# Two weight units in halves at the opening, squares folded between weight splits, and another order of ScalarE and VectorE in the scan and the last feed-forward pair

## The chip, the cores and the metric

The kernel runs on one core of a Trainium2 chip. The metric is the device time of one execution in microseconds. The kernel before was timed three times: 883.58, 883.80 and 884.14 us, median 883.8 us.

## The reference

Two transformer blocks over 256 tokens of width 1024, all in float32. The change touches only the first block, its opening, its scan and its feed-forward part; in the second block it renames semaphores.

```
h = rms_norm(x, norm_mix_pre);  z = h @ w_in
zq, zf_f, zf_b, zi, zg, zu, zv, ga, gb = split(z)

# scan mixer, both directions, 8 heads of 128
q = silu(zq);  v = zi
f = lb + (1 - lb) * sigmoid(zf);   k = (1 - lb) * sigmoid(-zf)
S_t = diag(f_t) S_{t-1} + k_t v_t^T;   o_t = S_t^T q_t
a = rms_norm(o_fwd + o_bwd) * silu(zg)

# spatial gating: tokens mixed inside chunks of 128
b = gelu(zu) * (w_s @ layer_norm(gelu(zv)) + b_s)

merged = sigmoid(ga) * (a @ w_a) + sigmoid(gb) * (b @ w_b)
x = x + rms_norm(merged @ w_out)
h2 = rms_norm(x)
x = x + rms_norm((silu(h2 @ w_gate) * (h2 @ w_up)) @ w_down)
x = x + (p @ w_ple) * sigmoid(x @ w_ple_gate)
```

The second block follows: an input projection, two attentions, an output projection and a feed-forward part with a squared relu.

## The kernel before, in words

**Units.** All weights stream through four slots of `raw` as units of 128 x 2048 floats (1 MB). ScalarE copies each unit to `whi` in the matmul's shortened float type (`split_hi`, L425), VectorE writes the rest `raw - whi` to `wlo` (`split_lo`, L834), and TensorE makes each product three times: high by high, low by high, high by low (`mm3`, L1523 to L1525, 48 matmuls of 256 columns per unit). SyncE loads unit u+4 as soon as unit u's last matmul has counted up `unit_used`. ScalarE and VectorE split three units ahead (`ahead(u)` splits u+3). The order on each engine is the order in which its block of code is written; nothing is scheduled.

**Opening.** SyncE sends the parameters, the first half of x, unit 0 in two halves, the second half of x and then whole units. ScalarE and VectorE make high and low parts of the gained x (`gained_hi` L450, `gained_lo` L883) and of the halves of unit 0 (L472, L913). TensorE multiplies unit 0 in two halves (`first_products`, L1631 to L1637) and then unit 1 (L1650 to L1652): 48 matmuls of 512 columns in all. ScalarE squares x (L478), VectorE folds the eight tiles of squares to one (`fold`, L867), TensorE sums them over partitions (`norm_stats`, L1613), GpSimd raises to the power -0.5 (L338), VectorE spreads the factors (L862), and TensorE broadcasts them (`norm_bc`, L1619). After that unit 2 and the further ones follow (`two_tiles`). A chain of small VectorE instructions normalises zv (from L940) for `spatial_mix` (L1666), which stands between units 4 and 5. GpSimd issues four loads (lnr, sgw, sgb, lvl) once unit 1 has landed.

**Scan.** Units 4 to 15 give q, f and k for two groups of four heads (g = 0 and 1). The scan is a tree of levels: for each level ScalarE copies alternating key rows to `Kc` (`both_ways`, L506), TensorE multiplies them with the queries (L1692), VectorE selects the results into S (L988) and multiplies the decays into the queries (`tree_update`, L964 and L970), and GpSimd does so to the keys (`keys_update`, L354). `prep` on VectorE makes the key sum `ksum` (L977), which level 0 (L1680) and the first Kc copy need, and the first decayed queries (L980). Level 8 is the last (L1699).

**Feed-forward.** Eleven pairs of hidden tiles: a gate unit, an up unit and a down unit each. For a pair VectorE scales the gate (L1138), ScalarE takes silu (L614), VectorE multiplies by the factors and by the up result (L1145, L1150), ScalarE and VectorE split the hidden tile (L618, L1154), and TensorE multiplies it by the down unit (L1776 to L1778). The splits of three coming units stand between these steps. Behind the last pair come copies and mean squares of the token-major results and a diagonal of factors (L1087, L1098), which the turning matmuls use (L1781).

Of the kernel before, what the change touches and what calls it, by code (L numbers as in the profile page):

```python
# [172 lines left out]
def build_blocks(nc, w, xT, pT, par, cst, lvl, sgw, sgb, lnr, rel, oneh, maskb, pos, out):  # L173
    scratch = nc.dram_tensor("bias_scratch", [HEADS, 512], F32, kind="Internal").ap()
    ctx = ExitStack()
    with ctx:
# [84 lines left out]
        zi = view(72, 8, D)  # L261
        t1 = view(80, 4, 512)
# [43 lines left out]
        def _(sp):  # L306
            sp.dma_start(par_s[:, :], par).then_inc(sem("par_in"), 16)
            sp.dma_start(x[:, 0:4, :], xT[:, 0:4, :]).then_inc(sem("x_in"), 16)
            for half in range(2):
                cols = slice(half * UNIT // 2, (half + 1) * UNIT // 2)  # L310
                sp.dma_start(raw[:, 0, cols], w[stored(0)][:, cols]).then_inc(sem(f"raw_half{half}"), 16)
            sp.dma_start(x[:, 4:8, :], xT[:, 4:8, :]).then_inc(sem("x_in2"), 16)
# [11 lines left out]
        def _(pool):  # L324
            pool.dma_start(cst_s[:, :], cst).then_inc(sem("cst_in"), 16)
            pool.wait_ge(sem("raw_in1"), 16)
# [3 lines left out]
            pool.dma_start(lvl_s[:, :, :], lvl).then_inc(sem("lvl_in"), 16)  # L330
            nc.gpsimd.memset(half_s[:, :], -0.5).then_inc(sem("half"), 1)
            pool.wait_ge(sem("half"), 1)
# [7 lines left out]
            token_factors(0)  # L340

# [48 lines left out]
            def head_factors(name, a, n):  # L390

                pool.wait_ge(sem(name + "_eps"), 1)
                nc.gpsimd.tensor_tensor(rh[:, a:a + n], ms[:, a:a + n], half_s[:, 0:1].broadcast_to([P, n]), ALU.pow)\
                    .then_inc(sem(name + "_fac"), 1)
                pool.wait_ge(sem(name + "_fac"), 1)
# [13 lines left out]
            for j in range(4):  # L409
                rotate(j)  # L410
                head_factors(f"sq{j}", 48 + 4 * j, 4)
# [6 lines left out]
        def _(act):  # L418
            A = nc.scalar.activation

            def split_hi(u):

                slot = u % SLOTS
                act.wait_ge(sem(f"raw_in{slot}"), 16 * (u // SLOTS + (slot > 0)))
# [39 lines left out]

            act.wait_ge(sem("par_in"), 16)
            act.wait_ge(sem("x_in"), 16)
            for k in range(2):
                gained_hi("n1", "mix_pre", 0, k)
            for half in range(2):
                cols = slice(half * UNIT // 2, (half + 1) * UNIT // 2)  # L470
                act.wait_ge(sem(f"raw_half{half}"), 16)
                A(whi[:, 0, cols], raw[:, 0, cols], ACT.Copy).then_inc(sem(("first_hi", "hi_ready")[half]), 1)  # L472
# [152 lines left out]
            for j in range(1, PAIRS1):  # L625
# [191 lines left out]
        def _(dve):  # L817
# [88 lines left out]

            dve.wait_ge(sem("par_in"), 16)
            dve.wait_ge(sem("x_in"), 16)
            for half in range(2):
                cols = slice(half * UNIT // 2, (half + 1) * UNIT // 2)  # L910
                gained_lo("n1", "mix_pre", 0, half)
                dve.wait_ge(sem(("first_hi", "hi_ready")[half]), 1)
                V.tensor_tensor(wlo[:, 0, cols], raw[:, 0, cols], whi[:, 0, cols].bitcast(F32), ALU.subtract)\  # L913
                    .then_inc(sem(("first_lo", "lo_ready")[half]), 1)
            dve.wait_ge(sem("x_in2"), 16)
            for k in range(2, 4):
                gained_lo("n1", "mix_pre", 0, k)
            split_lo(1)
            dve.wait_ge(sem("norm_sq"), 2)
            fold(sq1)  # L920

            gam = par_s[:, PAR["gamma"]:PAR["gamma"] + 16]
            V.tensor_tensor(lb[:, 0, :], gam, gam, ALU.subtract).then_inc(sem("gam_sub"), 1)
# [1413 lines left out]
```

## Time and profile before

| what | us |
|---|---|
| median of three timed runs | 883.8 |
| the profiled execution itself | 882.76 |
| its span, first to last instruction | 881.0 |
| TensorE busy (matmul) | 859.0 (98%) |
| VectorE busy | 581.9 (66%) |
| ScalarE busy | 443.7 (50%) |
| GpSimd busy | 91.9 (10%) |

A timeline row gives the start, the length, the engine, the line, the operation, what is written and read, the shape and the number of instructions merged in the row; in square brackets stands how long the engine had been idle before it and what ended that. A float32 product (not in the shortened type) leaves two matmul records each in the trace.

### The profile page before, as it was taken

The numbers are of one execution on the slowest core, as the hardware profiler recorded it, in microseconds if no ns is written. First come the engines' busy times: TensorE is split into PE (matmuls) and PEld (weight loads), VectorE is DVE, ScalarE is ACT, GpSimd is POOL, SyncE is SP. The second block draws the span as 40 slices with busy tenths as digits, with TensorE's granted clock in tenths as the row PEclk, the third lists the DMA queues.
The fourth block names the chain that finished last, engine by engine and source line by source line (L and its number), as shares of the span: only waits on it lengthen the run. The fifth ranks groups of instructions, "written<-read, shape, count | busy, mean of one in ns | idle before, by whom it ended". The sixth has DMA issues, their size and how long they took to land. (4 is left out here: it accounts for less than half of the span.)

```text
span 881.0 us, 15077 instructions
## 1 busy us (share of the span) xinstructions
PE 859.0 (98%) x6628; PEld 826.1 (94%) x6628; DVE 581.9 (66%) x703; ACT 443.7 (50%) x516; POOL 91.9 (10%) x71
## 2 busy tenths in 40 slices
PE   5999999999999999999999999999999999999997
PEld 4999998999999899999999899998998999999997
DVE  5866896676676587555565687688787765555454
ACT  6578764553344475344333564466556644444440
POOL 1000541452000000000000001000441000000000
PEclk9999999999999999999999999999999999999999
DMA  9554344244355455555555536544221455555551
GB/s 334 191 183 151 137 144 142 98 144 144 109 191 176 148 203 172 177 184 189 187 191 192 184 124 225 164 176 144 97 96 50 164 176 187 191 191 176 171 180 49
DMA packets 21121, 143.90 MB, mean 163 GB/s; under 512 B 2578, under 2 KB 2594, under 8 KB 4416
## 3 DMA queue, kind: packets, MB, share of 16 engines
q1 hardware_dynamic: 20016, 139.51, 45.4%
q0 software_dynamic: 1040, 3.43, 1.1%
q8 instruction: 52, 0.85, 0.4%
q14 instruction: 13, 0.11, 0.0%
HBM read 141.87 MB, written 1.06 MB: 162 GB/s over the span
## 5 line engine op out<-in xcount | busy, mean ns | idle before, releaser
L1523 PE MATMUL ps<-xh,whi 128*128 128x256 f32 x1656 | 475.4, 287 | 1.3 <-DVE wlo L834 1.0
L1524 PE MATMUL ps<-xl,whi 128*128 128x256 f32 x1656 | 468.9, 283 | 0.0
L1525 PE MATMUL ps<-xh,wlo 128*128 128x256 f32 x1656 | 468.8, 283 | 0.0
L834 DVE TENSOR_TENSOR wlo<-raw,whi 128x2048 fp32r<-128x2048 f32 x130 | 297.4, 2290 | 133.7 <-ACT whi L425 133.0
L425 ACT ACTIVATE whi<-raw 128x2048 fp32r<-128x2048 f32 x130 | 247.9, 1910 | 165.6 <-DMA raw<-w 165.5
L1523 PEld LDWEIGHTS ps<-xh,whi 128*128 128x128 f32 x1656 | 317.8, 192 | 4.4 <-issue 1.7
L1524 PEld LDWEIGHTS ps<-xl,whi 128*128 128x128 f32 x1656 | 317.9, 192 | 0.5
L1525 PEld LDWEIGHTS ps<-xh,wlo 128*128 128x128 f32 x1656 | 317.7, 192 | 0.0
L354 POOL TENSOR_TENSOR work<-work 128x512 f32<-128x512 f32 x28 | 55.5, 2001 | 126.2 <-ACT work L506 99.4
L618 ACT ACTIVATE xh<-work 128x512 fp32r<-128x512 f32 x27 | 17.1, 632 | 81.0 <-DVE work L1486 41.2
L893 DVE TENSOR_TENSOR work<-ps,bcs 128x512 f32<-128x512 f32 x34 | 23.4, 689 | 21.9 <-PE ps L1525 20.0
L1776 PE MATMUL ps<-whi,xh 128*128 128x512 f32 x88 | 34.5, 392 | 0.8 <-DVE xl L1154 0.8
L1777 PE MATMUL ps<-whi,xl 128*128 128x512 f32 x88 | 34.4, 391 | 0.0
L1778 PE MATMUL ps<-wlo,xh 128*128 128x512 f32 x88 | 34.3, 389 | 0.0
L456 ACT ACTIVATE work<-work 128x512 f32<-128x512 f32 x26 | 16.4, 631 | 29.6 <-DVE work L893 29.4
L1154 DVE TENSOR_TENSOR xl<-work,xh 128x512 fp32r<-128x512 f32 x27 | 18.7, 693 | 18.8 <-ACT xh L618 18.8
L1692 PE MATMUL ps<-work 128*128 128x128 f32 x224 | 29.4, 285 | 1.0 <-ACT work L506 1.0
L1692 PEld LDWEIGHTS ps<-work 128*128 128x128 f32 x224 | 28.1, 192 | 1.4 <-ACT work L506 1.2
L370 POOL TENSOR_TENSOR nt<-nt,half_s 128x1 f32<-128x1 f32 x4 | 2.2, 552 | 250.6 <-DVE nt L1093 250.6
L988 DVE COPY_PREDICATED work<-lvl_s,ps 128x512 f32<-128x512 int32 x28 | 19.1, 739 | 13.6 <-PE ps L1692 12.6
L338 POOL TENSOR_TENSOR rtok<-eps_s,half_s 128x2 f32<-128x2 f32 (+1 forms) x5 | 3.9, 770 | 225.8 <-DVE eps_s L860 225.8
L883 DVE SCALAR_TENSOR_TENSOR xl<-x,par_s,xh 128x256 fp32r<-128x256 f32 x32 | 13.9, 481 | 10.3 <-ACT xh L450 10.3
(264 smaller groups left out, 927.0 us busy)
## 6 DMA issues: line engine op xcount, KB each, us to landing
raw<-w SPq DMA_DIRECT2D x130, 1024.0 KB, 4.9
x<-xT SPq DMA_DIRECT2D x2, 512.0 KB, 6.7
raw<-w SPq DMA_DIRECT2D x2, 512.0 KB, 7.6
work<-bias_scratch POOLq DMA_DIRECT2D x1, 1024.0 KB, 7.8
out<-x SPq DMA_DIRECT2D x4, 256.0 KB, 2.3
work<-lnr POOLq DMA_DIRECT2D x1, 512.0 KB, 6.0
work<-sgw POOLq DMA_DIRECT2D x1, 512.0 KB, 6.7
lvl_s<-lvl POOLq DMA_DIRECT2D x1, 448.0 KB, 9.2
```

Source lines behind the costliest of these rows:

```text
L354: ins = nc.gpsimd.tensor_tensor(v, v, pair[:, :, 1 - d:2 - d].broadcast_to([P, n, half]), ALU.mult)
L425: A(whi[:, slot, :], raw[:, slot, :], ACT.Copy).then_inc(sem("hi_ready"), 1)
L834: V.tensor_tensor(wlo[:, slot, :], raw[:, slot, :], whi[:, slot, :].bitcast(F32), ALU.subtract)\
L893: V.tensor_tensor(dst, two(ps[u % RING][:, :]), factors_by_tile(2), ALU.mult).then_inc(sem(f"evac{u % RING}"), 1)
L988: V.copy_predicated(H["S"][:, s, :, s * P:(s + 1) * P], lvl_s[:, lv - 1, :].unsqueeze(1).broadcast_to([P, 4, P]), ps[3 + 2 * g + s][:, :]. ...
L1523: mm(out, hi, xh[:, tile, :], start=start, stop=False, skip_group_check=skip)
L1524: mm(out, hi, xl[:, tile, :], start=False, stop=False, skip_group_check=skip)
L1525: return mm(out, wlo[:, slot, at:at + width], xh[:, tile, :], start=False, stop=stop, skip_group_check=skip)
L1692: last = mm(banks[s][:, h * P:(h + 1) * P], H["Kc"][:, h, s * P:(s + 1) * P], alternating(H["Q"], lv, 1, h * T + s * P, P), start=True, st ...
L1776: mm(o, xh[:, base + kk, xs], whi[:, slot, wc], start=first, stop=False, skip_group_check=True)
L1777: mm(o, xl[:, base + kk, xs], whi[:, slot, wc], start=False, stop=False, skip_group_check=True)
L1778: return mm(o, xh[:, base + kk, xs], wlo[:, slot, wc], start=False, stop=end, skip_group_check=True)
```

## The change

The opening:

- the parameters are loaded by ScalarE's DMA queue, x is SyncE's first load, and unit 1, too, comes in two halves;
- VectorE sets 128 x 128 elements of `work` to one, ScalarE runs a one-element Copy and TensorE 26 float32 products of that tile with itself into a bank that nobody reads, before anything has landed;
- TensorE multiplies both units by `first_products`, in four quarters ordered by part (high, low of x, low of the weights);
- VectorE splits unit 1 in halves; its fold of the squares is cut in two around the split of unit 2; the split of unit 3 comes ahead of the norm's factors;
- `norm_stats` moves from between units 1 and 2 into the middle of unit 2;
- GpSimd's loads of lnr, sgw and sgb wait for unit 3 instead of unit 1, and lvl comes behind the norm's factors and unit 4;
- ScalarE loads the Gelu table by a one-element Gelu before the split of unit 4.

The scan: `ksum` is a step of its own. For group 0 VectorE scales unit 10 before the splits of units 12 and 13, and ScalarE makes the first Kc copy before it activates unit 10. For group 1 VectorE does the decayed queries after the seventh level of group 0 instead of before it.

The feed-forward part: in the last pair both engines split the second of the three coming units behind the hidden tile instead of ahead of it.

In the second block several semaphores become one with a count (`sq`, `red`), with the same waits.

```diff
 sync
-            sp.dma_start(par_s[:, :], par).then_inc(sem("par_in"), 16)
             sp.dma_start(x[:, 0:4, :], xT[:, 0:4, :]).then_inc(sem("x_in"), 16)
-            for half in range(2):
...
-            for u in range(1, UNITS):
+            for u in range(2):
+                for half in range(2):
+                    cols = slice(half * UNIT // 2, (half + 1) * UNIT // 2)
+                    sp.dma_start(raw[:, u, cols], w[stored(u)][:, cols]).then_inc(sem(f"raw_half{2 * u + half}"), 16)
+                if u == 0:
+                    sp.dma_start(x[:, 4:8, :], xT[:, 4:8, :]).then_inc(sem("x_in2"), 16)
+            for u in range(2, UNITS):
 gpsimd
-            pool.wait_ge(sem("raw_in1"), 16)
+            nc.gpsimd.memset(half_s[:, :], -0.5).then_inc(sem("half"), 1)
+            pool.wait_ge(sem("half"), 1)
+            pool.wait_ge(sem("raw_in3"), 16)
...
-            pool.dma_start(lvl_s[:, :, :], lvl).then_inc(sem("lvl_in"), 16)
...
             token_factors(0)
+            pool.wait_ge(sem("raw_in0"), 16)
+            pool.dma_start(lvl_s[:, :, :], lvl).then_inc(sem("lvl_in"), 16)
 scalar
+            act.dma_start(par_s[:, :], par).then_inc(sem("par_in"), 16)
+            act.wait_ge(sem("warm_set"), 1)
+            A(warm[:, :], wtile[:, 0:1], ACT.Copy)
...
-            split_hi(1)
+            first_hi(1)
             for k in range(2):
                 A(sq1[:, 4 * k:4 * k + 4, :], x[:, 4 * k:4 * k + 4, :], ACT.Square).then_inc(sem("norm_sq"), 1)
             split_hi(2)
+            split_hi(3)
...
-            ahead(U_ZV)
-            ahead(U_ZV + 1)
-            filled(U_ZV + 1)
+            act.wait_ge(sem("half"), 1)
+            A(warm[:, :], half_s[:, 0:1], ACT.Gelu)
+            split_hi(4)
...
-                    if kind == "level" and 1 <= lv <= 7 and (g, lv) != (1, 1):
+                    if kind == "level" and 1 <= lv <= 7 and lv + g > 1 and (g, lv) != (1, 1):
                         both_ways(g, lv)
                 if not U_ZI <= u < U_GA:
                     ahead(u)
+                if u == U_Q[1]:
+                    both_ways(0, 1)
...
                 silu_pair(j)
-                split_hi(u + 1 + RING)
+                if j < PAIRS1 - 1:
+                    split_hi(u + 1 + RING)
                 hidden_hi(j, "hid", 2 * (j % 2), j % 2)
+                if j == PAIRS1 - 1:
+                    split_hi(u + 1 + RING)
 vector
+            V.memset(wtile, 1.0).then_inc(sem("warm_set"), 1)
...
+            link(V.tensor_tensor(sq1[:, 0:4, :], sq1[:, 0:4, :], sq1[:, 4:8, :], ALU.add))
             split_lo(2)
+            link(V.tensor_tensor(sq1[:, 0:2, :], sq1[:, 0:2, :], sq1[:, 2:4, :], ALU.add))
+            V.tensor_tensor(sq1[:, 0, :], sq1[:, 0, :], sq1[:, 1, :], ALU.add).then_inc(sem("folded"), 1)
+            split_lo(3)
+            norm_factors("n1", 0)
+            split_lo(4)
...
                 if u == U_Q[1] - 1:
                     gates(0, 1, 1)
+                    hgrn_dve("ksum", 0, 0)
                     hgrn_dve("prep", 0, 0)
+                    scaled(U_Q[1], G[1]["q"][:, 0:2, :])
                 for step in behind.get(u, ()):
                     hgrn_dve(*step)
+                if u == U_ZI + 1:
+                    hgrn_dve("prep", 1, 0)
                 ahead(u)
...
                 if u == U_ZI:
-                    hgrn_dve("prep", 1, 0)
+                    hgrn_dve("ksum", 1, 0)
 tensor
+            pe.wait_ge(sem("warm_set"), 1)
+            for _ in range(26):
+                mm(ps[3][:, 0:P], wtile, wtile, start=True, stop=True)
             first_products(0)
             used(first_products(1))
-            arrived(U_ZV + 1)
...
+            first_products(2)
+            used(first_products(3))
             pe.wait_ge(sem("cst_in"), 16)
-            norm_stats("n1", sq1)
...
+                    if u == U_ZU:
+                        steps.append(lambda: norm_stats("n1", sq1))
```

VectorE at the opening, before; `xl` and `wlo` are low parts, `work` holds the squares, `lb` the scan's lower bounds:

```order
L883 SCALAR_TENSOR_TENSOR xl<-x,par_s,xh 128x256 x4
L834 TENSOR_TENSOR wlo<-raw,whi 128x2048
L867 TENSOR_TENSOR work<-work 128x1024
L867 TENSOR_TENSOR work<-work 128x512
L867 TENSOR_TENSOR work<-work 128x256
L923 TENSOR_TENSOR lb<-par_s 128x16
L834 TENSOR_TENSOR wlo<-raw,whi 128x2048
```

The same place now:

```order
L931 TENSOR_TENSOR wlo<-raw,whi 128x1024
L942 TENSOR_TENSOR lb<-par_s 128x16
L944 TENSOR_TENSOR work<-work 128x1024
L850 TENSOR_TENSOR wlo<-raw,whi 128x2048
L946 TENSOR_TENSOR work<-work 128x512
L947 TENSOR_TENSOR work<-work 128x256
L850 TENSOR_TENSOR wlo<-raw,whi 128x2048
L876 TENSOR_SCALAR eps_s<-ps 128x2
L878 COPY rx<-rtok 128x256
L850 TENSOR_TENSOR wlo<-raw,whi 128x2048
```

The split of unit 2 (the first 128x2048 row) now stands inside the fold, and that of unit 3 ahead of the norm's factors.

ScalarE in the scan at units 9 to 11, before; the 128x4x128 row copies level 0 out of PSUM, and the 128x1024 row behind it is the first Kc copy:

```order
L425 ACTIVATE whi<-raw 128x2048
L456 ACT_TABLE_LOAD
L456 ACTIVATE work<-work 128x512
L514 ACTIVATE work<-ps 128x4x128 x2
L506 ACTIVATE work<-work 128x1024
L425 ACTIVATE whi<-raw 128x2048
```

The same place now:

```order
L428 ACTIVATE whi<-raw 128x2048
L517 ACTIVATE work<-work 128x1024
L459 ACT_TABLE_LOAD
L459 ACTIVATE work<-work 128x512
L525 ACTIVATE work<-ps 128x4x128 x2
L428 ACTIVATE whi<-raw 128x2048
```

The Kc copy moved ahead of the table load, of the activation of unit 10 and of the copies of level 0.

VectorE in the last feed-forward pair, before; the 128x512 rows are the hidden tile's steps, the first L1087 row is the first copy behind the pair:

```order
L1138 TENSOR_TENSOR work<-ps,bcs 128x512
L834 TENSOR_TENSOR wlo<-raw,whi 128x2048 x2
L1145 TENSOR_TENSOR work<-work,bcs 128x512
L1150 TENSOR_TENSOR work<-work,ps 128x512
L1154 TENSOR_TENSOR xl<-work,xh 128x512
L834 TENSOR_TENSOR wlo<-raw,whi 128x2048
L1087 COPY work<-ps 128x512
```

The same place now:

```order
L1168 TENSOR_TENSOR work<-ps,bcs 128x512
L850 TENSOR_TENSOR wlo<-raw,whi 128x2048
L1175 TENSOR_TENSOR work<-work,bcs 128x512
L1180 TENSOR_TENSOR work<-work,ps 128x512
L1184 TENSOR_TENSOR xl<-work,xh 128x512
L850 TENSOR_TENSOR wlo<-raw,whi 128x2048 x2
L1117 COPY work<-ps 128x512
```

One weight split changed sides of the hidden tile's three steps.

## Rows read from the trace of the kernel before

**Rows 1.** The page, part 1: busy time of each engine.
```profile
PE 859.0 (98%) x6628; PEld 826.1 (94%) x6628; DVE 581.9 (66%) x703; ACT 443.7 (50%) x516; POOL 91.9 (10%) x71
```

**Rows 2.** Timeline of TensorE, from the first product to unit 5.
```profile
10.05 2.05 PE L1631 MATMUL ps<-whi,xh 128*128 128x512 f32 x4 [10.05 <-ACT whi L472]
...
14.84 1.09 PE L1631 MATMUL ps<-whi,xh 128*128 128x512 f32 x4
...
18.15 0.50 PE L1650 MATMUL ps<-whi,xh 128*128 128x512 f32 x1 [0.39 <-DVE wlo L834]
...
23.72 0.50 PE L1613 MATMUL ps<-cst_s,work 128*128 128x1 f32 x4
...
30.29 0.37 PE L1523 MATMUL ps<-xh,whi 128*128 128x256 f32 x1
...
41.98 1.97 PE L1666 MATMUL ps<-work 128*64 128x128 f32 x32
```

**Rows 3.** Timeline of the other engines at the opening.
```profile
0.74 0.38 SPq L307 DMA_DIRECT2D par_s<-par  x1
1.18 0.42 SPq L308 DMA_DIRECT2D x<-xT  x1
...
8.87 1.04 ACT L472 ACTIVATE whi<-raw 128x1024 fp32r<-128x1024 f32 x1
...
13.85 1.92 ACT L425 ACTIVATE whi<-raw 128x2048 fp32r<-128x2048 f32 x1 [0.77 <-DMA raw<-w]
...
15.68 1.99 ACT L478 ACTIVATE work<-x 128x1024 f32<-128x1024 f32 x2
...
18.01 2.40 DVE L867 TENSOR_TENSOR work<-work 128x1024 f32<-128x1024 f32 x3
...
29.95 1.41 DVE L940 BATCH_NORM_STATS2 nt<-work 128x6 f32<-128x512 f32 x2
...
38.03 0.69 DVE L893 TENSOR_TENSOR work<-ps,bcs 128x512 f32<-128x512 f32 x1
```

**Rows 4.** The page, part 6: the load of lnr, size and time to landing.
```profile
work<-lnr POOLq DMA_DIRECT2D x1, 512.0 KB, 6.0
```

**Rows 5.** Windows: behind the last product; TensorE's granted clock stands last but two.
```profile
878.00:881.00 3.00, 0.00 (x0) 0.00 (x0) 0.00 (x0) 0.00 (x0) 0.00 (x0) 0.50 0.24 90
```

**Rows 6.** Timeline of the scan of group 0, units 9 to 11.
```profile
77.88 1.23 DVE L977 TENSOR_TENSOR work<-work 128x1024 f32<-128x1024 f32 x1
79.02 2.35 DVE L980 TENSOR_TENSOR work<-work 128x1024 f32<-128x1024 f32 x2
...
79.89 1.28 ACT L456 ACT_TABLE_LOAD   x1
...
85.70 1.52 ACT L506 ACTIVATE work<-work 128x1024 f32<-128x1024 f32 x1
...
87.27 2.92 PE L1692 MATMUL ps<-work 128*128 128x128 f32 x16 [1.04 <-ACT work L506]
```

**Rows 7.** Timeline at the end of group 0's levels.
```profile
130.79 5.14 POOL L354 TENSOR_TENSOR work<-work 128x512 f32<-128x512 f32 x2 [2.93 <-DVE work L970]
...
132.95 2.07 DVE L977 TENSOR_TENSOR work<-work 128x1024 f32<-128x1024 f32 x1
134.94 3.20 DVE L980 TENSOR_TENSOR work<-work 128x1024 f32<-128x1024 f32 x2
...
140.81 0.60 PE L1699 MATMUL ps<-work 128*128 128x128 f32 x3 [0.36 <-DVE work L964]
```

**Rows 8.** Timeline of the last feed-forward pair and what follows.
```profile
491.91 2.29 DVE L834 TENSOR_TENSOR wlo<-raw,whi 128x2048 fp32r<-128x2048 f32 x1 [3.15 <-ACT whi L425]
...
497.12 0.47 PE L1776 MATMUL ps<-whi,xh 128*128 128x512 f32 x1 [0.76 <-DVE xl L1154]
...
501.88 0.29 DVE L1098 TENSOR_SCALAR work<-cst_s,nt 128x128 f32<-128x128 f32 x1
...
502.65 1.95 PE L1781 MATMUL ps<-work 128*128 128x128 f32 x16
```

More of the change, by code:

```diff
@@ L462, in bc_copy, with first_hi @@
                 A(bcs[:, :], ps[7][:, T:2 * T], ACT.Copy).then_inc(sem("norm_bcs"), 1)
+            act.dma_start(par_s[:, :], par).then_inc(sem("par_in"), 16)
+            act.wait_ge(sem("warm_set"), 1)
+            A(warm[:, :], wtile[:, 0:1], ACT.Copy)
             act.wait_ge(sem("par_in"), 16)
             act.wait_ge(sem("x_in"), 16)
+            def first_hi(u):
+                for half in range(2):
+                    cols = slice(half * UNIT // 2, (half + 1) * UNIT // 2)
+                    act.wait_ge(sem(f"raw_half{2 * u + half}"), 16)
+                    A(whi[:, u, cols], raw[:, u, cols], ACT.Copy).then_inc(sem(("first_hi", "hi_ready")[half]), 1)
             for k in range(2):
                 gained_hi("n1", "mix_pre", 0, k)
[L469 to L472, printed above, removed]
+            first_hi(0)
             act.wait_ge(sem("x_in2"), 16)
@@ L975, in hgrn_dve @@
                 H = G[g]
+                if kind == "ksum":
+                    V.tensor_tensor(H["ksum"], H["K"][0], H["K"][1], ALU.add).then_inc(sem("ksum"), 1)
                 if kind == "prep":
-                    V.tensor_tensor(H["ksum"], H["K"][0], H["K"][1], ALU.add).then_inc(sem("ksum"), 1)
                     activated(U_Q[g] + 1)
@@ L1630, in first_products @@
                 for s, k in pairs:
-                    mm(o[s], xh[:, k, xs[s]], whi[:, 0, 512 * k:512 * k + 512], start=k == 0, stop=False)
-                pe.wait_ge(sem("act_lo"), half + 1)
+                    mm(o[s], xh[:, 2 * quarter + k, xs[s]], whi[:, u, wc[k]], start=quarter == 0 and k == 0, stop=False)
+                pe.wait_ge(sem("act_lo"), quarter + 1)
                 for s, k in pairs:
-                    mm(o[s], xl[:, k, xs[s]], whi[:, 0, 512 * k:512 * k + 512], start=False, stop=False)
@@ L1635, in first_products @@
-                pe.wait_ge(sem(("first_lo", "lo_ready")[half]), 1)
+                    mm(o[s], xl[:, 2 * quarter + k, xs[s]], whi[:, u, wc[k]], start=False, stop=False)
+                pe.wait_ge(sem(("first_lo", "lo_ready")[half]), u + 1)
                 for s, k in pairs:
-                    last = mm(o[s], xh[:, k, xs[s]], wlo[:, 0, 512 * k:512 * k + 512], start=False, stop=False)
+                    last = mm(o[s], xh[:, 2 * quarter + k, xs[s]], wlo[:, u, wc[k]], start=False, stop=quarter == 3 and k == 1)
@@ L1638, in first_products @@
                 return last
+            pe.wait_ge(sem("warm_set"), 1)
+            for _ in range(26):
+                mm(ps[3][:, 0:P], wtile, wtile, start=True, stop=True)
             first_products(0)
             used(first_products(1))
-            arrived(U_ZV + 1)
-            for s in range(2):
-                o = ps[(U_ZV + s) % RING][:, :]
-                for k in range(4):
-                    if s == 0 and k % 2 == 0:
-                        pe.wait_ge(sem("act_lo"), before("lo", "n1") + 3 + k // 2)
-                    xs = slice(s * P, (s + 1) * P)
-                    wc = slice(512 * k, 512 * k + 512)
-                    mm(o, xh[:, 4 + k, xs], whi[:, 1, wc], start=False, stop=False)
-                    mm(o, xl[:, 4 + k, xs], whi[:, 1, wc], start=False, stop=False)
-                    last = mm(o, xh[:, 4 + k, xs], wlo[:, 1, wc], start=False, stop=k == 3)
@@ L1653, in _ @@
-            used(last)
+            first_products(2)
+            used(first_products(3))
             pe.wait_ge(sem("cst_in"), 16)
-            norm_stats("n1", sq1)
             inside, behind = hgrn_schedule()
```

75 lines of the change are left out of this document (35 added, 40 removed).

## The prediction

> **What bounds the kernel now.** I read the page's busy times first. TensorE has matmuls in flight for 859.0 of 881.0 us, VectorE and ScalarE are far below that [rows 1]. So an edit pays only where it lets TensorE start sooner, run at a higher clock or not stand still, and the timeline of TensorE is the view to go by: what stands in its square brackets is all there is to win, apart from slow products. TensorE's first product starts at 10.05; from 14.84 on groups of four take 1.09 us instead of 2.05; it waits briefly at 18.15 [rows 2]. Then it waits for ScalarE's first Kc copy at 87.27 [rows 6], for VectorE at level 8 at 140.81 [rows 7] and for the last pair's hidden tile at 497.12 [rows 8]. These four places are the ones that the change touches. The idle time in a row is a little less than the loss: the four products at 14.84 take 1.09, while 24 products from 18.15 to 23.72 come 0.232 apart [rows 2], so a record lasts 1.09 - 3 x 0.232 = 0.39, or 0.16 beyond its spacing. I add 0.16 to each idle time. The weights arrive whenever a unit is used up, so loads move with TensorE and take nothing back; later stages move with it as a whole.
>
> **The start.** x was the second load, issued at 1.18; now it is the first, at 0.74 [rows 3]: 0.44 us. ScalarE copied the first half unit at 8.87 for 1.04 us [rows 3] and TensorE began 0.14 later. The x parts and the table load, which the one-element Copy puts into the empty wait, are then long done, so the landing decides, and I let it move by the 0.44: first product at 9.6. Bounds: 0 (the loads compete anyway, and the parameters now run on another queue beside x) to 1.0 (the half was not waited for, so it may have landed before 8.87).
>
> **The clock.** TensorE had done nothing before 10.05. The twelve products up to 14.84 would take 2.8 us at 0.232 and took 4.79; with slow ones at twice 0.232 that makes 8.7 slow products, about 4.0 us at 1.2 GHz and a loss of 2.0 [rows 2]. The new 26 products are float32, eight of which (16 records) take 1.95 [rows 8], so about 0.22 each, 0.44 at the lower level. If they start at about 1.1 (the first loads are issued at 0.74, and a small memset comes first), 4.0 us make 9 of them, and the other 17 take 3.7: done at 8.8, ahead of 9.6. So they cost nothing and give back the 2.0. Bounds: 2.0 gained to about 3 lost, the latter below. As to the time between 8.8 and 9.6: in this trace the granted clock is at 0.50, the 1.2 GHz level, in the window from 878 to 881, in which TensorE has no product [rows 5]. The Trainium skill's page "TensorE: Matmul & The Clock Gate", section "Part 1: The HAM clock gate (the "warmup" mystery)", says that the throttled state is the default and that activity releases it; by that rule the slow products at 10.05 and the low clock at the end are one thing, and warm products help as long as the pause behind them is short.
>
> **The opening's sum.** 48 products of two units at 0.232 take 11.1 us: from 9.6 to 20.7, without a wait, since the halves' copies (1.04 each) and VectorE's halves keep ahead of quarters of 2.8 us each. Unit 2 must be split by then. Unit 1 landed at 13.85, so its second half lands at 13.4; behind the first half's copy ScalarE has it at about 14.7. The squares take 1.99, the copy of unit 2 1.92 [rows 3]: 18.6. VectorE's split takes 2.29 [rows 8]: 21.0 with a signal. The fold used to stand as one piece of 2.40 [rows 3]; cut in two, its first part lies in the wait for that copy. So unit 2 starts at 21.0, a wait of 0.3. From 23.72 to 30.29 lay norm_stats, unit 2 and norm_bc, 6.57 [rows 2]; the same three are there now in another order: unit 3 at 27.6 instead of 30.29. **Gain 2.7.** Without the move of norm_stats it would wait for the second part of the fold; in the middle of unit 2, at 23.9, the fold (done at about 22.2) is ready. Bounds of the opening: 0.7 (start not earlier, products slow) to 3.7.
>
> What is late next: the zv chain on VectorE. It began at 29.95 behind two splits, so the factors were done 4.6 earlier, 1.65 behind the start of norm_stats at 23.72 [rows 2, 3]. Now: 23.9 + 1.65, one split of 2.29, about 0.9 for the four lower-bound steps that were ahead before: 28.8. From 29.95 to the scaling at 38.03 it took 8.1 [rows 3], so it ends at 36.9. spatial_mix, at 41.98 [rows 2] less 2.7, wants it at 39.3. Room 2.4, cost nothing. GpSimd's loads now wait for unit 3 (about 18.5: unit 1 at 13.4 and two units of some 2.5 us each); lnr took 6.0 [rows 4], so it is there at 24.5, ahead of 28.8. Those on lvl are needed only at 87.
>
> **The scan.** ksum ends at 79.1, ScalarE is free at 79.89 (where the table load starts), and the copy takes 1.52 [rows 6]: Kc at 81.4 instead of 87.22. The table load, 1.28, moves behind it to 82.7, the queries are decayed by 81.4, and level 0's copies come in time, as they did just before 85.70. TensorE is at level 1 at 87.27 - 1.04 - 0.16 = 86.07 and finds all. **Gain 1.2**; bounds 0 and 1.2. At the end of group 0, 3.20 us of decayed queries for group 1 [rows 7] leave from ahead of the seventh selection, which then ends around 137.8; GpSimd's last keys are done at 130.79 + 5.14 = 135.9, TensorE comes at 140.3. **Gain 0.36 + 0.16 = 0.5**; bounds 0 and 0.5. The moved queries are wanted only after unit 20.
>
> **The last pair.** VectorE's split at 491.91 takes 2.29 and waited for a landing; the hidden tile stood behind it. Now the tile's steps start with the up unit's end and are done at about 493, TensorE wants them at 497.12 - 0.76 - 0.16 = 496.2. The gain is 0.92, if the next chain follows: the diagonal was ready at 501.88 + 0.29 = 502.17 and used at 502.65 [rows 8], room 0.48, and the second split now stands next to the third ahead of it. Both fit, since the third waits for its load anyway. **Gain 0.85**, bounds 0.48 and 0.92. The renamed semaphores have the same waits: 0.
>
> **Sum.** 2.7 + 1.2 + 0.5 + 0.85 = 5.25 us. The profiled execution, 882.76 with 1.8 around its span, becomes 877.5. The median of the timed runs is 1.0 above the profiled one, so I predict 883.8 - 5.25 = 878.6.
>
> **Rivals.**
>
> *The first products are slow all the same* (the clock has fallen again by 9.6, or rises late). For it: nothing in the trace shows the clock across a pause of a microsecond or two at the start, and it is low without products [rows 5]. Against it: the pause is short. 48 products end at 9.6 + 11.1 + 2.0 = 22.7, unit 3 starts at 29.3, gain 1.0, total 3.55: 880.3.
>
> *The 26 products run at 1.2 GHz to their end.* Then 26 x 0.44 = 11.4, end at 12.5, and the real ones finish between 23.6 and 25.6; unit 3 starts at 30.2 to 32.2, a gain of 0.1 to a loss of 1.9. With the middle, -0.9, the total is 1.65: 882.2. Against it: the clock rose after 4 us in the opening before.
>
> *The scan hands its wait on.* GpSimd's first keys now run from 81.4 beside VectorE's splits of units 12 and 13. Side by side, the key sum took 2.07 instead of 1.23 and the queries 3.20 instead of 2.35, and GpSimd 5.14 [rows 6, 7]. The split of unit 12 could go from 82.0 to 84.3 and must be done by 87.8, so a stretch of 0.85 is harmless, and I keep 1.7 for the scan; if it isn't, because selections start late level after level, the 1.7 is lost: 880.3. The Trainium skill's page "SBUF — State Buffer", section "SBUF: two separate sides", has VectorE with two SBUF inputs and GpSimd exclude each other for a whole instruction; by that rule the split would wait up to one of GpSimd's two key steps, half of 5.14, and end at 86.9, still in time but 0.9 from the edge.
>
> *Slower: lnr lands late.* Its load is issued later than before, next to units 4 and 5. Each microsecond of landing beyond 28.8 + 2.4 = 31.2 holds up the zv chain and, at spatial_mix, TensorE. The kernel is slower by what can be told from 38.3 on (31.2 + 5.25 + 1.8), that is if 0.5 MB take 20 us and not 6.0 [rows 4]; at 40 it is 883.8 - 5.25 + 8.8 = 887.3. Nothing speaks for that length, as the queue's megabytes come in about 2.5 us each.
>
> **Numbers.** Forecast with its mechanism, 877.8 to 879.4: 0.62. Slow first products 0.10, the scan's wait handed on 0.10, slow warm products 0.05, late lnr 0.02. The rest, 0.11, is halves of the terms' bounds: an earlier start than 9.6 (down to 877) or none, and small new waits (up to 881). Range 877.2 to 881.0; below and above it about 0.1 each. This kernel's time is told from no change at about 0.2%, 1.8 us: faster 0.93, same 0.05, slower 0.02.
>
> **What would show it.** The first product at 9.6 and four of them in 1.09 already; no wait among the four quarters; unit 2 at 21.0, unit 3 at 27.6; spatial_mix 2.7 earlier without a wait; no idle time at level 1, level 8 and in the last down unit; the turning products at most 0.1 late. Wrong would be: groups of 2.05 again, a start above 10, VectorE as releaser of unit 2 by more than 1 us, a wait at a later level, or the end less than 4.5 us earlier although those waits are gone.

## Result and profile after

The new kernel takes 876.13 us (median of 4 runs, 875.93 to 876.31) against 883.69 us for the kernel before, timed beside it: ratio 0.992, 95% interval 0.9908 to 0.9932, 7.6 us less. Forecast were 878.6 with a range from 877.2, so direction and places were right and the gain was 2.3 us too small. Its profiled execution took 875.93 with a span of 874.1: 6.8 us less than the profiled execution before.

The page's busy times, to be held against [rows 1]:

```profile
PE 863.9 (99%) x6680; PEld 832.1 (95%) x6680; DVE 583.5 (67%) x705; ACT 445.1 (51%) x519; POOL 93.9 (11%) x71
```

TensorE is busy 4.9 us longer in a span 6.8 us shorter: the products of ones fill 7.6 us that were idle, and the slow products at the start, about nine by the prediction's own working, are gone. The timeline of TensorE at the opening, answering to [rows 2]:

```profile
1.06 7.64 PE L1671 MATMUL ps<-work 128*128 128x128 f32 x52 [1.06 <-DVE work L923]
8.62 1.16 PE L1660 MATMUL ps<-whi,xh 128*128 128x512 f32 x4
...
11.43 1.07 PE L1660 MATMUL ps<-whi,xh 128*128 128x512 f32 x4
...
18.68 1.07 PE L1666 MATMUL ps<-wlo,xh 128*128 128x512 f32 x4
...
23.09 0.50 PE L1639 MATMUL ps<-cst_s,work 128*128 128x1 f32 x4
...
38.45 1.97 PE L1687 MATMUL ps<-work 128*64 128x128 f32 x32
```

The real products start at 8.62, four take 1.16 or 1.07 us from the first group on, and no idle time stands among the quarters. The other engines there, answering to [rows 3]:

```profile
0.74 0.40 ACTq L468 DMA_DIRECT2D par_s<-par  x1
0.74 0.38 SPq L308 DMA_DIRECT2D x<-xT  x1
...
5.20 1.71 ACT L453 ACTIVATE xh<-x,par_s 128x256 fp32r<-128x256 f32 x4 [2.53 <-DMA par_s<-par]
...
7.42 1.06 ACT L479 ACTIVATE whi<-raw 128x1024 fp32r<-128x1024 f32 x1 [0.51 <-DMA raw<-w]
...
17.70 2.29 DVE L850 TENSOR_TENSOR wlo<-raw,whi 128x2048 fp32r<-128x2048 f32 x1 [0.35 <-ACT whi L428]
...
20.14 0.36 PE L1549 MATMUL ps<-xh,whi 128*128 128x256 f32 x1 [0.38 <-DVE wlo L850]
...
26.77 0.36 PE L1549 MATMUL ps<-xh,whi 128*128 128x256 f32 x1
```

ScalarE now really waits for the first half unit (0.51) and starts its copy at 7.42 instead of 8.87. That needs the early table load too: its parts of x run from 5.20 to 6.9, and with the 1.28 us of the table load [rows 6] ahead of them they would have ended at 8.2, an estimate from these rows. Unit 2 waits 0.38 + 0.16 for its split; unit 3 starts at 26.77 instead of 30.29, 3.5 us earlier.

In the scan (answering to [rows 6, 7]) and behind the last pair ([rows 8]), the same timeline:

```profile
82.55 2.83 PE L1713 MATMUL ps<-work 128*128 128x128 f32 x16
...
135.48 0.72 PE L1720 MATMUL ps<-work 128*128 128x128 f32 x5
...
496.12 0.29 DVE L1128 TENSOR_SCALAR work<-cst_s,nt 128x128 f32<-128x128 f32 x1
...
496.55 2.02 PE L1804 MATMUL ps<-work 128*128 128x128 f32 x16 [0.22 <-DVE work L1128]
```

Levels 1 and 8 start without idle time, 4.7 and 5.3 us earlier than before. The last down unit has none either, but the turning products wait 0.22 + 0.16 for the diagonal.

TensorE's instructions, set side by side one by one in the two traces, give the account of the 6.8 us:

| place | forecast | found |
|---|---|---|
| opening, up to unit 3 | 2.7 | 3.5 |
| scan, levels 1 and 8 | 1.7 | 1.9 |
| last pair | 0.85 | 0.6 (1.0 less 0.45 at the turning products) |
| the rest, up to the last product | 0 | -0.1 |
| from the last product to the end of the span | 0 | 0.9 |

The remaining 0.7 us of the 7.6 is not between the two traces: the timed runs of the kernel before have their median 0.9 above its profiled run, those of the new one 0.2.

The traces show what the last row of the table goes with. The DMA view of the last output's transfer, from its issue to its landing, in the kernel before (877.4 to 880.6):

```profile
q14 instruction: 1, 0.01, 0.6%
out<-x SPq DMA_DIRECT2D x1, 256.0 KB, 3.2
```

with the scan's edits alone (875.1 to 877.7; the run is told of below):

```profile
q14 instruction: 1, 0.01, 0.7%
out<-x SPq DMA_DIRECT2D x1, 256.0 KB, 2.6
```

and in the new kernel (871.5 to 873.8), whose view has no line of `instruction` there:

```profile
q1 hardware_dynamic: 169, 0.28, 32.7%
out<-x SPq DMA_DIRECT2D x1, 256.0 KB, 2.3
```

One packet of 8 KB that loads instructions runs 0.31 us in the middle of the last output's transfer. Packet by packet, it starts 1.83 us behind the issue in the kernel before, and the output's last 4-byte packet comes only behind it, at 2.13; the landing takes 3.18 us. With the scan or the pair alone that small packet gets in just ahead of it, and the landing takes 2.58. In all nine profiles with the new opening the nearest such packet stands 4.3 to 4.4 us ahead of the issue, and the landing takes 2.28 to 2.34. This holds in all 14 profiles. No edit moved that packet alone, and why it costs more than its 0.3 us is not shown.

### The profile page after: what moved, and what is told of

It is laid out like the page before. It is cut to its first block, busy times and chain, and to the rows that moved or that the text cites. A ratio compares the mean times of both kernels' runs of the same rounds, so it can differ in the third digit from the quotient of the medians.

```text
span 874.1 us, 15188 instructions
## 1 busy us (share of the span) xinstructions
PE 863.9 (99%) x6680; PEld 832.1 (95%) x6680; DVE 583.5 (67%) x705; ACT 445.1 (51%) x519; POOL 93.9 (11%) x71
## 4 chain that ended last, share of the span: by engine, by line
PE 86%; DVE 7%; ACT 4%; DMA 1%; issue 1%; SPq 0%; POOL 0%; DVEq 0%
PE ps L1549 22%; PE ps L1550 21%; PE ps L1551 21%; PE ps L1713 3%; PE ps L1800 2%; PE ps L1799 2%; PE ps L1801 2%; DVE wlo L850 2%; ACT whi L428 1%; PE ps L1615 1%; PE ps L1621 1%; PE ps L1618 1%; DMA x<-xT 1%; ACT work L732 1%; PE ps L1804 1%
## 5 line engine op out<-in xcount | busy, mean ns | idle before, releaser
L357 POOL TENSOR_TENSOR work<-work 128x512 f32<-128x512 f32 x28 | 57.3, 2067 | 119.0 <-DVE work L1004 52.8
L517 ACT ACTIVATE work<-work 128x1024 f32<-128x1024 f32 x14 | 16.1, 1147 | 8.2 <-POOL work L357 3.5
```

The lines of the kernel that those rows point to most:

```text
L357: ins = nc.gpsimd.tensor_tensor(v, v, pair[:, :, 1 - d:2 - d].broadcast_to([P, n, half]), ALU.mult)
```

## Experiments

The numbers below stand against the kernel before on the same chip; it had a median of 882.85 to 883.17 there, with runs from 881.6 to 885.7.

**The opening alone.** The new kernel with the scan's and the last pair's edits taken back, in the code of ScalarE and of VectorE:

```diff
-                if u == U_Q[1]:
-                    both_ways(0, 1)
...
-                if j < PAIRS1 - 1:
-                    split_hi(u + 1 + RING)
+                split_hi(u + 1 + RING)
                 hidden_hi(j, "hid", 2 * (j % 2), j % 2)
-                if j == PAIRS1 - 1:
-                    split_hi(u + 1 + RING)
...
-                    hgrn_dve("ksum", 0, 0)
                     hgrn_dve("prep", 0, 0)
-                    scaled(U_Q[1], G[1]["q"][:, 0:2, :])
...
```

> The new kernel with the scan and the last feed-forward pair in the old order: the opening (and the semaphore names) alone. Theory A (three independent places, and the rest of the 7.6 us is how long the last output took to land): first product at 8.6, norm_stats on TensorE about 3.5 us earlier than before, waits of 1.2 and 0.5 us in the scan and 0.9 at the last pair back in place; the end 3.5 us earlier, 880.2. Theory B (the opening gives its surplus to a later stage, or the shorter tail belongs to it): 879.3 or less, with the last output landing 2.3 us after its issue instead of 3.2.

Measured: 879.13 us (878.77 to 879.34), 3.7 less, ratio 0.9951 (0.9938 to 0.9964). TensorE's start:

```profile
1.06 8.83 PE L1656 MATMUL ps<-work 128*128 128x128 f32 x52 [1.06 <-DVE work L918]
9.64 1.17 PE L1645 MATMUL ps<-whi,xh 128*128 128x512 f32 x4
```

The waits in the scan and at the last pair are back (1.43, 0.51 and 1.14 us). The first product came at 9.64, not 8.6: the 26 products of ones took 1.2 us longer than in the new kernel, which at half rate means that the clock rose about 2.4 us later, and they ran until 9.6 although ScalarE's half was ready at 8.7. TensorE's lead on the kernel before is 3.1 us at unit 3 and 2.6 at the last product; the last output landed in 2.29 us. So theory B was right about the tail, which is 0.9 of the gain and belongs to this opening's program, and wrong about later stages, which got nothing.

**The scan alone.**

```diff
+                if u == U_Q[1]:
+                    both_ways(0, 1)
...
+                    hgrn_dve("ksum", 0, 0)
                     hgrn_dve("prep", 0, 0)
+                    scaled(U_Q[1], G[1]["q"][:, 0:2, :])
...
+                if u == U_ZI + 1:
+                    hgrn_dve("prep", 1, 0)
```

> The kernel before with the scan's new order alone. Theory A: the opening as before, no wait at level 1 and level 8, TensorE's last product 1.85 us earlier, time 881.9. Theory B (what shows as a scan gain needs the earlier VectorE of the new opening): 0.5 to 1.2 us, 882.5 to 883.2.

Measured: 880.56 us (879.81 to 881.01), 2.3 less, ratio 0.9968 (0.9955 to 0.9981). Both waits are gone with the old opening in place, against theory B. TensorE gains 1.95 us in the scan in this profile, near theory A's 1.85; the shorter landing of the last output (2.58 instead of 3.18) adds 0.6. The runs lie within 1.2 us of each other where the kernel before has 4.

**The last pair alone.** VectorE's part, ScalarE's is the same:

```diff
+                if j < PAIRS1 - 1:
+                    split_lo(u + 1 + RING)
                 hidden(j, j % 2, u + 1, (u + 1) % RING)
                 hidden_lo(j, j % 2, "hid", 0)
+                if j == PAIRS1 - 1:
+                    split_lo(u + 1 + RING)
```

> The kernel before with the last feed-forward pair's new order alone. Theory A: the wait of the last down unit (0.92) goes, one of about 0.35 appears at the turning products behind it, since VectorE's diagonal comes 0.35 late; net 0.6, 883.1. Rival: the diagonal is on time when the opening is the old one, net 0.9, 882.8.

Measured: 881.67 us, ratio 0.9992 (0.998 to 1.0003), no clear change; seven runs lie at 880.98 to 881.67 and five at 883.2 to 884.8. By itself this part cannot be told from the scatter by the times. In its trace the wait at the last down unit is gone and the turning products start 0.35 us late, a net 0.65, as theory A has it. Its profiled run, 883.22, is of the upper kind, and shows what one of these is:

```profile
88.17 3.70 PE L1698 MATMUL ps<-work 128*128 128x128 f32 x16 [2.38 <-ACT work L506]
```

```profile
80.00:87.50 7.50, 5.79 (x50) 5.58 (x48) 7.50 (x7) 3.76 (x6) 0.00 (x0) 1.00 0.41 139
88.25:91.66 3.41, 3.41 (x17) 3.41 (x17) 0.00 (x0) 2.19 (x2) 2.99 (x2) 0.50 0.50 209
```

The first row is the timeline's at level 1, the others are windows (TensorE's granted clock is the third number from the end). The wait for the first Kc copy is 2.5 us instead of 1.2 [rows 6], and behind it the clock is at 0.50, 1.2 GHz, for 3.41 us; the same 16 records take 3.70 instead of 2.92 us.

The longer wait has a source 25 us earlier. ScalarE's copy of one weight unit, in the kernel before, in its second profile (e10_before, below) and here:

```profile
61.14 1.90 ACT L425 ACTIVATE whi<-raw 128x2048 fp32r<-128x2048 f32 x1
```

```profile
62.33 1.92 ACT L425 ACTIVATE whi<-raw 128x2048 fp32r<-128x2048 f32 x1 [0.55 <-DMA raw<-w]
```

```profile
62.03 1.92 ACT L425 ACTIVATE whi<-raw 128x2048 fp32r<-128x2048 f32 x1 [1.25 <-DMA raw<-w]
```

The same load, issued at 55.7, 55.8 and 55.2, took 4.9, 6.5 and 6.8 us to land. TensorE did not notice, since the splits are three units ahead, but in e10_before VectorE stays 1.2 us behind the first profile from that unit's split to the scaling of unit 10, which ScalarE's activation and copies wait for ahead of the Kc copy. So the old order handed a late load on to level 1.

**The new kernel again,** unchanged, beside the three above.

> The new kernel once more, with its own profile, beside the kernel before. Theory A: TensorE's last product is again 5.9 us earlier than before's, while the landing of the last output varies between about 2.3 and 3.2 us from profile to profile; time 876.2 to 877.0, 6.5 to 7.6 us below the kernel before. Theory B (the short tail is the kernel's own): last landing 2.3 us again and 7.5 us below.

Measured: 876.09 us (875.90 to 876.17), 6.8 less, ratio 0.9916 (0.9902 to 0.9931). First product at 8.79; the last output landed in 2.29 us, as theory B has it, and the time lies between the two theories. One part alone gave 3.7, 2.3 and 1.2 by the medians (the last not to be told from none), 7.2 together, the whole 6.8. That they add up is in part luck: each has a shorter landing of the last output in it (0.9, 0.6 and 0.6 us), which the whole has once, the runs of the first were held up by the products of ones in its profile, and the kernel before scatters.

**The parameters ahead of x again.**

```diff
+            sp.dma_start(par_s[:, :], par).then_inc(sem("par_in"), 16)
             sp.dma_start(x[:, 0:4, :], xT[:, 0:4, :]).then_inc(sem("x_in"), 16)
...
-            act.dma_start(par_s[:, :], par).then_inc(sem("par_in"), 16)
```

> The new kernel with the parameters loaded by SyncE ahead of x again. Theory A (x second in the queue costs more than its issue time, since 128 small rows go ahead of it): x lands at 5.5 to 5.9 instead of 5.0, the first half unit at 8.2 to 8.8 instead of 7.5, first product at 9.5, time 877.0 (0.9 above the new kernel's 876.1). Rival (only the 0.44 us between the two issues counts): first product at 9.1, time 876.5.

Measured: 877.25 us (876.64 to 877.84), ratio 0.9929 (0.9914 to 0.9945) to the kernel before, 1.2 more than the new kernel. (The new kernel was timed on another chip than this and the next three; the kernel before has 882.89 on this one and 882.85 on that.) The copy of the first half and the first product:

```profile
8.65 1.06 ACT L479 ACTIVATE whi<-raw 128x1024 fp32r<-128x1024 f32 x1 [1.50 <-DMA raw<-w]
...
9.85 1.15 PE L1660 MATMUL ps<-whi,xh 128*128 128x512 f32 x4 [0.52 <-ACT whi L479]
```

A queue place of 0.43 us moved ScalarE's start on the first half by 1.2 (8.65 against 7.42 here; 7.3 to 7.7 in all seven other profiles with the parameters on ScalarE's queue). The half landed at 8.62 against 7.40; with the parameters ahead of x it lands at 8.2 to 8.8 in six profiles, without at 7.3 to 7.7 in eight. So the rival's 0.44 is too small, and theory A's price holds. Its reason, the small rows, is not shown: the edit moved the whole load, and nothing tells its size from its place.

**No products of ones, and ten of them.**

```diff
-            pe.wait_ge(sem("warm_set"), 1)
-            for _ in range(26):
-                mm(ps[3][:, 0:P], wtile, wtile, start=True, stop=True)
```

> The new kernel without the 26 products of ones on TensorE. Theory A (they buy the clock): the first product at 8.6 as now, some ten products twice as long, unit 2 starts 1.4 to 2 us later (a wait of 0.55 there is covered), time 877.5 to 878.1, and the runs spread by more than 0.5 us again. Rival (the granted clock rises soon anyway or unit 2's split binds): at most 876.8.

```diff
-            for _ in range(26):
+            for _ in range(10):
```

> The new kernel with 10 products of ones instead of 26, which end at about 5.2 and leave a pause of 3.4 us ahead of the first real product. Theory A (a short pause does no harm): 876.1 as with 26. Rival (the clock falls in the pause, the prediction's rival of slow first products): the first real products take 2.05 us per four, 877.5 to 878.1 as without any.

Measured: 877.59 us without (876.98 to 878.19), ratio 0.9933 (0.9917 to 0.9948), and 877.07 with ten (876.88 to 877.87), ratio 0.9928 (0.9911 to 0.9945); 1.5 and 1.0 more than with 26, and both scatter by 1 us. The intervals overlap that of 26 products (0.9902 to 0.9931), but all twelve runs lie above the nine with 26. TensorE without them:

```profile
8.73 2.04 PE L1660 MATMUL ps<-whi,xh 128*128 128x512 f32 x4 [8.73 <-ACT whi L479]
10.58 1.75 PE L1663 MATMUL ps<-whi,xl 128*128 128x512 f32 x4
12.17 1.09 PE L1666 MATMUL ps<-wlo,xh 128*128 128x512 f32 x4
```

and with ten:

```profile
1.06 4.64 PE L1671 MATMUL ps<-work 128*128 128x128 f32 x20 [1.06 <-DVE work L923]
8.81 2.05 PE L1660 MATMUL ps<-whi,xh 128*128 128x512 f32 x4 [3.11 <-ACT whi L479]
10.65 1.91 PE L1663 MATMUL ps<-whi,xl 128*128 128x512 f32 x4
12.36 1.62 PE L1666 MATMUL ps<-wlo,xh 128*128 128x512 f32 x4
13.81 1.09 PE L1660 MATMUL ps<-whi,xh 128*128 128x512 f32 x4
```

Ten products (4.64 us, the whole at the lower level) and a pause of 3.1 us left the real ones as slow as if there had been none: theory A of that run fell. But its rival is not shown either: the clock had not risen before the pause, so it could not fall in it. Whether ten were too few or the pause too long these runs cannot tell. The 26 buy about 1.5 us because the clock rises while they run. The Trainium skill's page "TensorE: Matmul & The Clock Gate", section "Part 1: The HAM clock gate (the "warmup" mystery)", calls the throttled state the default that activity releases; by that rule the slow groups here are expected, and these rows agree.

**norm_stats between units 1 and 2 again.**

```diff
             used(first_products(3))
             pe.wait_ge(sem("cst_in"), 16)
+            norm_stats("n1", sq1)
...
-                    if u == U_ZU:
-                        steps.append(lambda: norm_stats("n1", sq1))
```

> The new kernel with norm_stats between units 1 and 2 again. Theory A (the cut fold ends at 21.05): TensorE waits from 19.6 to 21.1 for the fold, unit 2 starts at 21.5 instead of 20.1 but holds no norm_stats, so 1.0 us is lost: 877.1. Rival (the wait for unit 2's split would have been there anyway and covers it): 876.3.

Measured: 877.11 us (876.89 to 877.89), ratio 0.9929 (0.9913 to 0.9944), 1.0 more than the new kernel.

```profile
9.59 1.17 PE L1660 MATMUL ps<-whi,xh 128*128 128x512 f32 x4
...
21.13 0.58 PE L1639 MATMUL ps<-cst_s,work 128*128 128x1 f32 x4 [0.39 <-DVE work L947]
```

Again the products of ones ran late, to 9.6; had the real ones started at 8.6, TensorE would only have waited longer for the fold, which follows from VectorE's split and not from TensorE, and ends at 21.0 in both programs. So the 1.0 us is the price of the place of norm_stats, as theory A has it.

**Filling the wait at level 1.** The kernel before, with five float32 products on a constant (ten records) ahead of TensorE's wait for Kc:

```diff
                     elif lv <= 7:
+                        if (g, lv) == (0, 1):
+                            idle_products(5, 5)
                         pe.wait_ge(sem("Kc"), 7 * g + lv)
```

> The kernel before, with five float32 products of the identity (1.1 us) into an idle bank while TensorE waits for the first Kc copy at level 1. They take nothing away and give no result. Theory A (the slower of the two clusters of the kernel before, 883.2 to 885.7 against 881.6 to 882.6, are executions in which the clock falls in that wait): the upper cluster goes, all runs within 1.5 us, median near 882.2 or below. Rival (the clusters come from the opening's slow products or the loads): two clusters as before.

**The kernel before, again.**

> The kernel before once more, with its own profile. Theory A: the first half unit lands at 8.2 to 8.8, first product 9.5 to 10.1, level 1's wait 1.2 to 2.5 us, and where the time is 883.2 or more the granted clock is 0.5 for 3.4 us there. Rival: the same wait in a slow and a fast execution, the difference in the opening.

Measured: with the filler 882.83 us (881.51 to 883.98, 11 runs), ratio 0.9993 (0.9984 to 1.0002), without it 883.95 (881.76 to 884.80, 12 runs) and 883.17 (881.81 to 885.51, 23 runs). Level 1 with the filler, then without:

```profile
85.66 1.28 PE L1607 MATMUL ps<-cst_s 128*128 128x128 f32 x10
86.99 2.92 PE L1694 MATMUL ps<-work 128*128 128x128 f32 x16
```

```profile
88.46 2.92 PE L1692 MATMUL ps<-work 128*128 128x128 f32 x16 [2.09 <-ACT work L506]
```

The two ratios show no clear change of time. But every run's mean granted clock is known. With the filler it is 0.999 or 1.000 in all 11 runs, and one of them is above 883.9 (883.98). Without it 13 of the 35 runs are above 883.9; their clock is 0.997 or 0.998 in 12 and 0.999 in the one that was profiled (883.96), while the runs up to 883.5 have 0.998 or more. The low clock behind the last product alone makes 0.998 [rows 5]; 0.997 stands in 12 of the 35 runs and in the profile with the fall at level 1. So falls of the clock go with most of the upper end, and none shows with the filler; that each of them is at level 1 is seen in one trace only. The filled kernel still spreads by 2.5 us where I had expected 1.5, and the profiled run at 883.96 has no fall, against theory A of that run: it has the long wait, 2.09 + 0.16, which is 1.05 of its 1.2 us above the first profile, and a clock that rose late in the opening, which is the other 0.15. Its first groups:

```profile
9.99 2.04 PE L1631 MATMUL ps<-whi,xh 128*128 128x512 f32 x4 [9.99 <-ACT whi L472]
11.83 1.91 PE L1634 MATMUL ps<-whi,xl 128*128 128x512 f32 x4
13.54 1.91 PE L1637 MATMUL ps<-wlo,xh 128*128 128x512 f32 x4
15.25 1.52 PE L1631 MATMUL ps<-whi,xh 128*128 128x512 f32 x4
```

Four groups are slow here, three in [rows 2]. Three things scatter the old kernel then, of which the new one shows none in its two profiles: the moment at which the clock rises, the length of the wait at level 1, and the fall behind it.

**Two further moves, with 26 and with 22 products of ones.**

```diff
-            for k in range(2):
-                A(sq1[:, 4 * k:4 * k + 4, :], x[:, 4 * k:4 * k + 4, :], ACT.Square).then_inc(sem("norm_sq"), 1)
+            A(sq1[:, 0:4, :], x[:, 0:4, :], ACT.Square).then_inc(sem("norm_sq"), 1)
             split_hi(2)
+            A(sq1[:, 4:8, :], x[:, 4:8, :], ACT.Square).then_inc(sem("norm_sq"), 1)
             split_hi(3)
...
+            split_lo(2)
             dve.wait_ge(sem("norm_sq"), 2)
             link(V.tensor_tensor(sq1[:, 0:4, :], sq1[:, 0:4, :], sq1[:, 4:8, :], ALU.add))
-            split_lo(2)
...
-                if j == PAIRS1 - 1:
-                    split_lo(u + 1 + RING)
-                split_lo(u + 2 + RING)
+                split_lo(u + (1 if j == PAIRS1 - 1 else 2) + RING)
...
             x_lo(3)
+            split_lo(U_PG + 1)
             ahead(U_PG - 1)
```

> The new kernel with two more moves: the second square of the first norm behind ScalarE's copy of unit 2 (and the fold's first step behind VectorE's split of it), and VectorE's split of unit 77 behind the turned results of the last pair. Theory A: the waits of 0.55 at unit 2 and 0.39 at the turning products go, 875.2 against 876.1. Rival (the fold is then late for norm_stats inside unit 2, or unit 77's split is late): 876.1 or more.

> The same with 22 products of ones instead of 26. Theory A (26 end after the first half unit is ready if the clock rises late, as in e1_open and e8_stats_between, and 22 don't): first product at 8.7 whatever the clock's moment, time as e11 where its clock rises early, up to 0.9 less where it rises late. Rival (the pause of 0.9 us lets the clock fall): 2 us more.

Measured: 875.49 us (875.18 to 876.09), ratio 0.9909 (0.9896 to 0.9922), and 875.19 us (875.09 to 875.21); the second, ratio 0.9905 (0.9892 to 0.9918) to the kernel before, is the best version by its median. The first is near theory A's 875.2. The timeline of the second:

```profile
1.06 6.54 PE L1670 MATMUL ps<-work 128*128 128x128 f32 x44 [1.06 <-DVE work L923]
8.79 1.17 PE L1659 MATMUL ps<-whi,xh 128*128 128x512 f32 x4 [1.19 <-ACT whi L479]
...
19.89 0.36 PE L1548 MATMUL ps<-xh,whi 128*128 128x256 f32 x1
...
495.92 1.95 PE L1803 MATMUL ps<-work 128*128 128x128 f32 x16
```

Both waits are gone, and a pause of 1.2 us after 22 products leaves the real ones at full rate, against the rival. That 22 protect from a late rise is not shown: the clock rose early in both profiled runs; only the runs are closer together (0.1 against 0.9 us).

## Why the prediction was wrong, step by step

The gains came at the places named and by the mechanisms named; what failed is the size of some terms, and two things that the sum took as unchanged.

**The start.** The first step that failed was "so the landing decides, and I let it move by the 0.44". Landing does decide, once the table load is out of the way, but it moved by 1.4 in the pair of profiles (8.79 to 7.40) and by 1.2 in the experiment on that edit alone, so the first product came 1.4 us earlier and not 0.44. The prediction priced a place in the queue by what it takes to issue. Part of the 1.4 is luck: the first product of the kernel before, at 10.05, is the latest of five profiles with the old opening (9.67 to 10.05). The forecast's bound (1.0) was too near as well.

**The clock.** Right in size: about nine of the first twelve products ran at half rate before, and now all groups of four take 1.1 us. The products of ones were done by 8.7, where 8.8 was forecast. Leaving them out made the first two real groups slow, 2.04 and 1.75 us, a loss of 1.6 of which unit 2's wait covers 0.5; 1.0 is left between the profiles and 1.5 between the medians, where 2.0 was forecast. The rival of slow first products in spite of them came true with ten, not with 26 and not with 22. That they can hold up the real ones by 1 us (e1_open, e8_stats_between) lay between the forecast and the rival that the prediction gave for it.

**The opening's sum.** The chain was right with everything 0.9 us earlier: unit 2 starts 0.5 behind the end of unit 1 because VectorE's split binds (forecast 0.3, at 21.0; found 20.14), norm_stats in the middle finds the fold ready, spatial_mix at 38.45 has no wait. The term came out at 3.5, inside its bounds of 0.7 to 3.7, 0.8 above the value taken.

**The scan.** 1.2 + 0.5 forecast, 1.9 found in the traces, and alone 2.3 by the timed medians, of which 0.6 is the landing of the last output. GpSimd and VectorE do hold each other up. The timeline of the new kernel around level 1:

```profile
77.98 1.50 POOL L357 TENSOR_TENSOR work<-work 128x512 f32<-128x512 f32 x1 [52.81 <-DVE work L1004]
78.41 3.22 DVE L850 TENSOR_TENSOR wlo<-raw,whi 128x2048 fp32r<-128x2048 f32 x1
79.44 3.57 POOL L357 TENSOR_TENSOR work<-work 128x512 f32<-128x512 f32 x1
81.55 3.61 DVE L850 TENSOR_TENSOR wlo<-raw,whi 128x2048 fp32r<-128x2048 f32 x1
```

Alone the update takes 1.5 us and the split 2.29. Here each ends about its own length behind the end of the one before it on the other engine: the update at 79.5, the split at 81.6, the update at 83.0, the split at 85.2. So they take turns, whole instruction by whole instruction, which is what the rule that the prediction quotes for its rival says. The rival priced one wait of up to 2.6 us; the two splits waited 2.2 together, 6.8 instead of 4.6 us, and TensorE did not notice. What the prediction did not see is that the wait differs between executions (1.2, 1.4, 2.25 and 2.5 us in four profiles with the old scan) and that the clock can fall behind it. One profile shows one of these cases, the mild one.

**The last pair.** The 0.92 went, but "Both fit" was wrong by about 0.4: the diagonal was ready at 496.41, wanted at 496.17 and used at 496.55, because the second split beside the third left VectorE no room. With one split moved behind the turned results (e11_fixed) the wait is gone. The bound of 0.48 allowed for it.

**The sum.** Two things were taken as unchanged. "The median of the timed runs is 1.0 above the profiled one" was carried over to the new kernel as if it were a constant of measuring; the new kernel's median is 0.2 above its profiled run. That is 0.7 us. The later runs of the kernel before show what lifts its median, the long wait and the lower clock; the three runs that the 883.8 comes from have no trace, so that it was the same in them is likely and not shown.

The largest single term is the 0.9 behind the last product, where the prediction let everything move with TensorE "as a whole". From the start of the last product the span goes on for 5.3 us in the old kernel's profiles (and with the filler), 4.7 with the scan or the pair alone, 4.4 to 4.5 with every new opening. TensorE, VectorE and the issue of the last output stand alike there and only its landing differs, with the packet of instructions that runs in it or not. The prediction's bounds had no room for that, and nothing in its rows pointed to it: as a gain of this change it is luck.

Together: 0.8 from the opening, 0.2 from the scan, -0.3 from the pair, -0.1 between there and the last product, 0.9 from the tail, 0.7 from the scatter of the old kernel, 2.3 in all within rounding. No rival came true, the slower one least.

## What to carry to other kernels

Price a load's place in the queue by landings, not by issue time: a load of 43 KB ahead of the first big ones took 0.43 us to issue and cost 1.2. If a kernel's timed runs lie above its profiled one, look for a wait whose length and clock vary, before taking the difference for an offset. Products that are to raise TensorE's clock must run until it has risen, and not past the first real one: 22 with 1.2 us to spare served here as well as 26, ten did not. Look at the DMA view of the last output before taking the end of a span for fixed.

## What the runs showed that was not expected

- Behind a wait of 2.5 us TensorE's granted clock was 0.50 for 3.41 us, and 16 records took 3.70 instead of 2.92 us; behind one of 2.25 us in another run it stayed at full rate.
- Ten products of ones, all at the lower level, then 3.1 us of pause: the real ones slow for three groups. Twenty-two and 1.2 us: full rate.
- 26 products of ones last 7.64 us in one profile and 8.83 in another whose program differs only from about 75 us on.
- A VectorE split of 2.29 us and a GpSimd key update of 1.5 us that meet take turns: 3.22 and 3.61 us for the two splits, 3.57 for the second update.
- One megabyte load landed after 4.9, 6.5 or 6.8 us in three profiles of the old order, and the wait at level 1, 25 us later, was 1.2, 2.25 or 2.5 us.
- The last output landed after 3.18 us with an 8 KB packet of instructions ahead of its last small packet, after 2.58 with that packet just behind it, and after 2.28 to 2.34 without one, in 14 of 14 profiles.
